# Attention: reciprocal sums applied to the exponents on GpSimd, value products with the latents stationary

## The reference

```python
def one_block(qi):
    s = jnp.einsum('bqhd,bkhd->bhqk', qi, k).astype(jnp.float32) * scale
    p = jax.nn.softmax(s, axis=-1).astype(v.dtype)
    return jnp.einsum('bhqk,bkhd->bqhd', p, v)
```

## Time and profile before

| What | Value |
|---|---|
| Median of 3 runs | 2599.09 us (2598.75 to 2599.27) |
| Profiled execution: its own time | 2597.56 us |
| Profiled execution: span | 2595.8 us |
| TensorE busy in the span | 93% |
| VectorE, ScalarE, GpSimd busy | 30%, 20%, 9% |
| Attention loop, layer 0 and layer 1 | about 303 us each (328 to 631, 1588 to 1891) |

### The profile page before, as it was taken

One profiled execution on the slowest core, in us unless ns is written; L12 is line 12 of the kernel. 1 busy time (PEld: TensorE's weight loads), 2 busy tenths in 40 slices (PEclk: granted clock), 3 DMA queues, 4 the chain that ended last, 5 costly groups with the idle time before them and its releaser, 6 DMA issues.

```text
span 2595.8 us, 33714 instructions
## 1 busy us (share of the span) xinstructions
PE 2427.0 (93%) x13939; PEld 1630.1 (63%) x13939; DVE 790.1 (30%) x1662; ACT 508.1 (20%) x1024; POOL 233.8 (9%) x371
## 2 busy tenths in 40 slices
PE   6999999999995899999979999999999949999994
PEld 4545566666443778888744455666654447887873
DVE  2401344454237211111142023454533451111112
ACT  2310121222233111101141002122213321111112
POOL 2000010100000121111200000000000002112121
PEclk8999999999997899999989999999999969999997
DMA  9100223311225588888840003330012258888887
GB/s 316 33 21 0 82 86 111 131 66 43 73 97 186 164 275 276 276 278 274 271 137 16 21 0 99 113 104 28 1 68 98 98 182 274 272 268 279 275 277 242
DMA packets 163074, 383.65 MB, mean 148 GB/s; under 512 B 12944, under 2 KB 23416, under 8 KB 162976
## 3 DMA queue, kind: packets, MB, share of 16 engines
q1 hardware_dynamic: 142944, 332.51, 37.4%
q0 software_dynamic: 20032, 49.77, 7.5%
HBM read 334.63 MB, written 47.61 MB: 147 GB/s over the span
## 4 chain that ended last, share of the span: by engine, by line
PE 91%; DVE 4%; DMA 2%; SPq 1%; ACT 1%; issue 1%; DVEq 0%; POOLq 0%; ACTq 0%
PE PS L1213 11%; PE PS L1220 11%; PE PS L1078 11%; PE PS L1240 9%; PE PS L815 8%; PE PS L975 7%; PE PS L908 6%; PE PS L769 5%; PE PS L758 5%; PE PS L957 4%; PE PS L920 4%; PE PS L1234 2%; PE PS L869 1%; PE PS L933 1%; PE PS L1198 1%; DVE top_i L1812 1%
## 5 line engine op out<-in xcount | busy, mean ns | idle before, releaser
L1213 PEld LDWEIGHTS PS<-r,ring 128*128 128x128 f32 x2048 | 285.8, 192 | 18.6 <-issue 18.6
L1213 PE MATMUL PS<-r,ring 128*128 128x160 f32 x2048 | 287.9, 302 | 3.5 <-ACT r L1457 3.5
L1078 PE MATMUL PS<-ring,mix 128*128 128x512 f32 x640 | 288.4, 598 | 1.2 <-DVE mix L1694 1.2
L1220 PE MATMUL PS<-r,ring 128*128 128x160 f32 x2048 | 283.4, 299 | 0.0
L1220 PEld LDWEIGHTS PS<-r,ring 128*128 128x128 f32 x2048 | 279.9, 190 | 0.0
L1240 PE MATMUL PS<-ring,r 128*128 128x512 f32 x512 | 228.3, 599 | 0.0
L908 PE MATMUL PS<-lat,r 128*128 128x512 f32 (+1 forms) x416 | 205.5, 579 | 5.4 <-ACT r L1342 2.7
L815 PE MATMUL PS<-r,ring 128*128 128x512 f32 (+1 forms) x576 | 208.4, 521 | 1.6 <-ACT r L1299 1.6
L975 PE MATMUL PS<-r 128*128 128x128 f32 x1536 | 202.2, 276 | 0.0
L975 PEld LDWEIGHTS PS<-r 128*128 128x128 f32 x1536 | 188.1, 192 | 18.9 <-issue 18.7
L1078 PEld LDWEIGHTS PS<-ring,mix 128*128 128x128 f32 x640 | 116.4, 190 | 129.7 <-issue 129.7
(11 more groups left out here) (259 smaller groups left out, 2171.8 us busy)
## 6 DMA issues: line engine op xcount, KB each, us to landing
ring<-in_w_gate_dram SPq DMA_DIRECT2D x32, 2048.0 KB, 9.9
ring<-in_w_up_dram SPq DMA_DIRECT2D x32, 2048.0 KB, 10.4
ring<-in_w_down_dram SPq DMA_DIRECT2D x32, 2048.0 KB, 9.6
ring<-in_w_ada_dram SPq DMA_DIRECT2D x21, 2048.0 KB, 20.9
x_dram<-r SPq DMA_DIRECT2D x20, 512.0 KB, 2.9
r<-x_dram SPq DMA_DIRECT2D x20, 512.0 KB, 4.1
r<-in_x_sample_dram SPq DMA_DIRECT2D x16, 512.0 KB, 4.1
ring<-in_w_in_dram SPq DMA_DIRECT2D x4, 2048.0 KB, 9.8
```

What stands on the lines that cost most here:

```text
L1078: ins = pe.matmul(psum(2 * (s % 2) + n, 512), mix[:, k, tile * P:(tile + 1) * P], W_OUT[n][:, k, :], start=(k == 0), stop=(k == KD - 1))
L1213: ins = pe.matmul(PS[:, b // 2, (b % 2) * 256:(b % 2) * 256 + SLOTS], W_G[:, k, b * P:(b + 1) * P], XST[par][:, k, :], start=(k == 0), sto ...
L1220: ins = pe.matmul(PS[:, 2 + b // 2, (b % 2) * 256:(b % 2) * 256 + SLOTS], W_U[:, k, b * P:(b + 1) * P], XST[par][:, k, :], start=(k == 0), ...
```

## The change

The reciprocals of the row sums are applied to the exponents, before they are turned, and no longer to the outputs. `invert_sum` only signals `inv_ready`; it stands after `row_max(n, 1)` for slot 0 and, for slot 1, after the first `copy_turned` of the next iteration. GpSimd multiplies `Pr[slot]` by `pinv` in place, 512 columns a round (two pieces of 256 for prompt tiles), and signals `p_scaled` for each round, on which `turn` waits. In `times_values` the operands are exchanged: `CKVT` is stationary, `PTr` moves, so that the result has the latent's numbers on partitions, as `mix` wants it. `scale_out`, `OS` and `turn_out` fall away, and `copy_out` copies each slot from bank 7. The stores of the gates move from GpSimd to SP, each behind the load of the piece of weights two later. The order of copies in the tail is adapted.

```diff
...
         SHUF = r2[:, 6144:7168]
-        OS = r2[:, 7168:7680].rearrange("p (s i c) -> p s i c", s=2, i=2)
         W_A = r2[:, 8192:9216].rearrange("p (h k c) -> p h k c", h=HEADS, k=2)
...
         o_summed = sem("o_summed")
-        o_scaled = sem("o_scaled")
-        o_turned = sem("o_turned")
+        inv_ready = sem("inv_ready")
+        p_scaled = sem("p_scaled")
         o_copied = sem("o_copied")
...
                 sp.wait_ge(ada_zeroed, l + 2)
+                def store_gate(i):
+                    la, n = ADA_ITEMS[l][i]
+                    if n in ADA_GATES:
+                        sp.wait_ge(ada_biased, 1 + ADA_AT[l] + i + 1)
+                        for g in range(2):
+                            for j in range(4):
+                                sp.dma_start(mod_dst[la, g, n, j:j + 1, :], ada_s[i % 2][32 * j + g:32 * j + g + 1, :])\
+                                    .then_inc(ada_stored[i % 2], 16)
                 for i, (la, n) in enumerate(ADA_ITEMS[l]):
...
                             .then_inc(ada_landed[i % 2], 16)
+                    if i >= 2:
+                        store_gate(i - 2)
+                for i in range(len(ADA_ITEMS[l]) - 2, len(ADA_ITEMS[l])):
+                    store_gate(i)
                 sp.wait_ge(ada_summed, 1 + ADA_AT[l + 1] - 1)
...
                 pool.memset(ada_b[1], 0.0).then_inc(ada_zeroed, 1)
-                for i, (la, n) in enumerate(ADA_ITEMS[l]):
-                    if n in ADA_GATES:
-                        pool.wait_ge(ada_biased, 1 + ADA_AT[l] + i + 1)
-                        for g in range(2):
-                            for j in range(4):
-                                pool.dma_start(mod_dst[la, g, n, j:j + 1, :], ada_s[i % 2][32 * j + g:32 * j + g + 1, :])\
-                                    .then_inc(ada_stored[i % 2], 16)
+                def scale_exponents(n, slot):
+                    pool.wait_ge(inv_ready, at(l, 2 * NI, 2 * n + slot + 1))
+                    for r in range(rounds_of(n)):
+                        if ITEMS[n][1] is PROMPT_TILES:
+                            for i in range(PT):
+                                e = Pr[slot][:, i * NP:(i + 1) * NP]
+                                ins = pool.tensor_scalar(e, e, pinv[:, 2 * slot + i:2 * slot + i + 1], None, ALU.mult)
+                        else:
+                            e = Pr[slot][:, 512 * r:512 * (r + 1)]
+                            ins = pool.tensor_scalar(e, e, pinv[:, 2 * slot:2 * slot + 1], None, ALU.mult)
+                        ins.then_inc(p_scaled, 1)
+                for n in range(NI):
+                    for slot in range(2):
+                        scale_exponents(n, slot)
                 for i in range(2):
...
                     k = turned(n, slot, r)
-                    pe.wait_ge(exp_done, at(l, 2 * NI, 2 * n + slot + 1))
+                    pe.wait_ge(p_scaled, at(l, ROUNDS, k))
                     if k > 1:
                         pe.wait_ge(pt_ready, at(l, ROUNDS, k - 1))
-                    if n and slot == 1 and r == 0:
-                        pe.wait_ge(o_copied, at(l, NI, n))
                     if slot == 0 and r == 0 and 0 < n <= len(ADA_ITEMS[l]):
...
                     if r == 0 and 2 * n + slot > 0:
-                        pe.wait_ge(o_scaled, at(l, 2 * NI, 2 * n + slot))
+                        pe.wait_ge(o_copied, at(l, 2 * NI, 2 * n + slot))
                     for j in range(4):
...
                             ins = pe.matmul(PS[:, 7, slot * 256 + (j // 2) * P:slot * 256 + (j // 2 + 1) * P],
-                                            PTr[slot][:, j, :], CKVT[:, j % 2, :], start=(j % 2 == 0), stop=(j % 2 == 1))
+                                            CKVT[:, j % 2, :], PTr[slot][:, j, :], start=(j % 2 == 0), stop=(j % 2 == 1))
                         else:
-                            ins = pe.matmul(PS[:, 7, slot * 256:slot * 256 + P], PTr[slot][:, k, :], CKVT[:, PT + k, :],
+                            ins = pe.matmul(PS[:, 7, slot * 256:slot * 256 + P], CKVT[:, PT + k, :], PTr[slot][:, k, :],
                                             start=(k == 0), stop=(k == 11))
...
                         ins.then_inc(o_summed, 1)
-
-                def turn_out(n):
-
-                    if n < 0:
-                        return
-                    tiles = PT if ITEMS[n][1] is PROMPT_TILES else 1
-                    pe.wait_ge(o_scaled, at(l, 2 * NI, 2 * n + 2))
-                    done = turned(n + 1, 1, 0) - 1 if n + 1 < NI else ROUNDS
-                    pe.wait_ge(pt_ready, at(l, ROUNDS, done))
-                    for slot in range(2):
-                        for i in range(tiles):
-                            c = (slot * tiles + i) * P
-                            ins = pe.transpose(PS[:, 6, c:c + P], OS[:, slot, i, :], ident[:, :])
-                    ins.then_inc(o_turned, 1)
...
                         rotary_scores(n, c)
-                    turn_out(n - 2)
                     times_values(n - 1, 0, 2)
...
                 n = NI - 1
-                pe.wait_ge(o_copied, at(l, NI, NI - 2))
+                pe.wait_ge(o_copied, at(l, 2 * NI, 2 * (NI - 2)))
                 pe.wait_ge(exp_done, at(l, 2 * NI, 2 * n + 1))
...
                 turn(n, 0, 2)
-                turn_out(n - 1)
                 times_values(n, 0, 1)
...
                 times_values(n, 1, 2)
-                pe.wait_ge(o_copied, at(l, NI, NI - 1))
+                pe.wait_ge(o_copied, at(l, 2 * NI, 2 * (NI - 1)))
                 value_heads(8)
                 value_heads(9)
-                turn_out(n)
-                pe.wait_ge(o_copied, at(l, NI, NI))
+                pe.wait_ge(o_copied, at(l, 2 * NI, 2 * NI))
                 value_heads(10)
...
                 pe.wait_ge(mod_ready, 2 * l + 2)
-                pe.wait_ge(o_scaled, at(l, 2 * NI, 2 * NI))
                 for s in range(NT):
...
-                def copy_out(n):
+                def copy_out(n, slot):
...
                     tiles, t0 = (PT, 0) if t is PROMPT_TILES else (1, t)
-                    act.wait_ge(o_turned, at(l, NI, n + 1))
-                    act.activation(mix[:, 2 * p:2 * p + 2, t0 * P:(t0 + tiles) * P],
-                                   psum(6, 2 * tiles * P).rearrange("p (h q) -> p h q", h=2), ACT.Copy)\
-                        .then_inc(o_copied, 1)
+                    act.wait_ge(o_summed, at(l, 2 * NI, 2 * n + slot + 1))
+                    act.activation(mix[:, 2 * p + slot, t0 * P:(t0 + tiles) * P], PS[:, 7, slot * 256:slot * 256 + tiles * P],
+                                   ACT.Copy).then_inc(o_copied, 1)
...
                 for n in range(NI):
-                    copy_out(n - 2)
+                    copy_out(n - 1, 0)
                     exponents(n, 0)
+                    copy_out(n - 1, 1)
                     exponents(n, 1)
                 copy_value_heads(0)
-                copy_out(NI - 2)
-                for m in (2, 4, 6, 8):
-                    copy_value_heads(m)
-                copy_out(NI - 1)
+                copy_value_heads(2)
+                copy_out(NI - 1, 0)
+                copy_value_heads(4)
+                copy_value_heads(6)
+                copy_out(NI - 1, 1)
+                copy_value_heads(8)
                 copy_value_heads(10)
...
                     dve.wait_ge(exp_done, at(l, 2 * NI, 2 * n + slot + 1))
-                    step(dve.reciprocal(pinv[:, c:c + m], psum_row[:, c:c + m]))
-
-                def scale_out(n, slot):
-
-                    if n < 0:
-                        return
-                    tiles = PT if ITEMS[n][1] is PROMPT_TILES else 1
-                    c = 2 * slot
-                    dve.wait_ge(o_summed, at(l, 2 * NI, 2 * n + slot + 1))
                     if n:
-                        dve.wait_ge(o_turned, at(l, NI, n))
-                    for i in range(tiles):
-                        ins = dve.tensor_scalar(OS[:, slot, i, :], PS[:, 7, slot * 256 + i * P:slot * 256 + (i + 1) * P],
-                                                pinv[:, c + i:c + i + 1], None, ALU.mult)
-                    ins.then_inc(o_scaled, 1)
+                        dve.wait_ge(p_scaled, at(l, ROUNDS, turned(n - 1, slot, rounds_of(n - 1) - 1)))
+                    dve.reciprocal(pinv[:, c:c + m], psum_row[:, c:c + m]).then_inc(inv_ready, 1)
...
                 for n in range(NI):
-                    for r in range(3):
-                        copy_turned(n - 1, 0, r)
-                    invert_sum(n - 1, 0)
-                    scale_out(n - 1, 0)
+                    copy_turned(n - 1, 0, 0)
+                    invert_sum(n - 1, 1)
+                    copy_turned(n - 1, 0, 1)
+                    copy_turned(n - 1, 0, 2)
                     copy_turned(n - 1, 1, 0)
...
                     copy_turned(n - 1, 1, 2)
-                    invert_sum(n - 1, 1)
                     row_max(n, 1)
+                    invert_sum(n, 0)
```

(6 more changed lines are left out.)

## The result

The changed kernel takes 2612.22 us (median of 6 runs, 2610.54 to 2613.7) against 2598.92 (6 runs) before: ratio 1.0052, 95% interval 1.0039 to 1.0065. That is 13.3 us or 0.52% slower: beyond the range, and on the side of rival 1. The profiled execution took 2610.54, its span 2608.5, which is 12.7 more than before's 2595.8; traces are compared by span.

What follows compares the result with a forecast made beforehand. TensorE, busy 98% of layer 0's attention window, was taken as the bound. Layer 0's -3.55 and layer 1's -0.95 made -4.5 us, 2597.56 to 2593.1; the median, 1.5 higher, was forecast at 2594.6, range 2590 to 2605.

Steps and rivals of the forecast that it cites:

- rival 1: GpSimd is slow: sixteen hand-overs carry the multiply, each 0.1 us costs 1.6; at 1.3 us, 2605; chance 0.2 for over 0.2% slower.
- the price of the multiply: GpSimd's `scale_exponents`, 128x512 elements a round: 0.65 us, bounds 0.5 and 1.3, from rows of a copy and selects.
- `turn_out`, 0.2 an item: TensorE's two transpositions between rotary scores and slot 0's last value products fall away: 0.2 us gained per item.
- Iteration 10, 1.0 each layer: `turn_out` just before `turn(9, 1, 0)`, which waited for the copy out of bank 6, falls away: 1.0 us gained.
- The hand-overs of 0.15 each: Semaphore hand-overs around GpSimd's multiply, 0.15 us in and 0.15 out, making 0.95 us from reciprocal to `turn`.
- The ordinary item's stall: Items without modulation product: first turn 6.71 us after `turn(.., 1, 1)`, not 6.16; stall 0.55, less 0.2 gain, +0.35 an item.
- Modulated items hidden until the multiply passes 2 us: Items with a modulation product: a cover of 1.4 us hides the multiply until it passes 2 us; they gain 0.2.
- First item +0.3: First, prompt item of each layer: reciprocal 0.2, hand-overs 0.3, two 256-column multiplies of 0.4 delay its turn: +0.3 us.
- Layer 1, iterations 9 and 10, +0.4: No modulation there: `turn(10, 0, 0)` at about 1777.7 against 1777.31, +0.4 us for both iterations, gain included.
- Bias add, 0.1 in iteration 2: The bias add follows one more reciprocal, at the first item and in iteration 10 of layer 0: +0.1 us each.
- The tail, -2.4 a layer: End of each layer: `turn_out` and two scalings fall away, 1.2 + 0.85 + 0.35 = 2.4 us gained, bounds 1.9 and 2.7.
- rival 3: Tail gives only two visible idle times (0.88, 0.47) because VectorE's copies bound it: 2596.7; with the forecast, chance 0.5 for no change.

Runs made afterwards that it cites:

- experiment 2: Changed kernel without GpSimd's multiplies and VectorE's wait for them; the turn waits for the exponents, reciprocals left out of the result: 2584.49 us, ratio 0.9949.
- experiment 3: Changed kernel with VectorE multiplying slot 0's first round right after its reciprocal, GpSimd all other rounds: 2590.0 us, ratio 0.9969.
- experiment 10: Changed kernel with scores (n, 0, 1) ahead of the first turn and VectorE multiplying slot 0's first round: 2591.94 us, ratio 0.9974.
- experiment 7: As experiment 3, but GpSimd's rounds of slot 0 wait for VectorE's multiply: 2591.46 us, ratio 0.9971.
- experiment 11: Changed kernel with GpSimd multiplying by the constant 1.0 instead of the column of reciprocals: 2607.58 us (one run).

## Why the prediction was wrong

**The step that failed** is the price of the multiply, "I take 0.65 us; the upper bound is twice that, 1.3". Its two anchors were a copy and a select, whose rows both ran near 0.85 ns an element; neither is arithmetic in f32. The multiply takes 1.566, above even the upper bound, which had no row behind it but a factor of two. That is over the 1 us that the prediction named as a sign of being wrong. The two sides of the sum show where the error sits: its gains add up to 13.6 us (the items, iteration 10 of each layer, the tails) and experiment 2 measured 13.5 in the attentions, while the waits and other costs were put at 9.1 and took 13.5 + 12.65 = 26.1. The Trainium skill (GPSIMD Engine Reference, sections 3.1 and 4.1) was right in direction, but its factor of two against VectorE is 3.2 in these runs, and its roughly line rate for one input holds for the copy, not for this multiply.

**The step that carries it** held. Rival 1 said that sixteen hand-overs carry the multiply. Ordered by the time from GpSimd's start to the first round's end, the spans are

| first round on GpSimd | us | span | two attentions, against before |
|---|---|---|---|
| none | 0 | 2581.5 | -13.5 |
| copy | 0.61 | 2590.3 | -7.0 |
| multiply by a constant (one run) | 1.49 | 2605.5 | +8.7 |
| multiply, as changed | 1.57 | 2608.5 | +12.65 |
| in two halves | 1.84 | 2612.5 | +17.9 |

From copy to multiply it is 18.2/0.96 = 19 us of span for a microsecond, against 16 forecast; the gain is gone at 0.61 + 5.5/19 = 0.90, where the rival said 0.93. By the attentions alone it is 20, and 0.95. Its formula at the true length gives -4.5 + 16 x 0.92 = +10.2; measured +12.7, of which 1.4 is the clock. The 4.0 us from the constant to the column are more than 0.07 us a hand-over can carry: 1.5 lie around iteration 11 of layer 1, where the clock fell in the latter alone, and an ordinary item grows by 0.13, 0.08 in its wait (1.07 to 1.15) and 0.05 from the turn to the next rotary scores (5.17 to 5.22).

**Point by point.**
- `turn_out`, 0.2 an item: 0.17 to 0.18. Right.
- Iteration 10, 1.0 each layer: there without GpSimd's step (15.59 against 16.57 in layer 0, 13.82 against 15.04 in layer 1), half of it kept by the changed kernel in layer 0 and none in layer 1. Right in what is removed, wrong in what is kept: the wait for the multiply comes in the same place.
- The reciprocal 5.76 after the turn: exact. The hand-overs of 0.15 each: 0.10 and 0.05, so 0.15 too dear together. The ordinary item's stall is therefore 0.55 + 0.92 - 0.15 = 1.32, by the timeline 7.47 - 6.16 = 1.31. Less 0.17 of gain, and 0.1 behind the restart (the next turn starts 1.55 after, 584.20, where it is 1.47 in experiment 2): +1.24 against +0.35.
- Modulated items hidden until the multiply passes 2 us: right as far as tried, 18.71 with every length up to 1.84.
- First item +0.3: +1.24, for it has two multiplies of 0.92 where 0.4 each was taken.
- Layer 1, iterations 9 and 10, +0.4: +3.4 (0.9 and 2.5). The 0.9 is the wait of 0.84 for the two multiplies of the prompt item 9, a hand-over that the prediction counted for the first item alone. The 2.5 is about the wait of 2.02 and the 1.4 of the clock, which no step of the prediction spoke of, less the 1.0 won.
- Bias add, 0.1 in iteration 2: +0.5, as the changed kernel keeps TensorE waiting 0.28 there for GpSimd; without GpSimd's step it is nothing (15.53 against 15.55).
- The tail, -2.4 a layer: -2.2 beside its own stall of 1.24. Right; rival 3 (1.35 a layer) is refuted.
- Operand exchange, stores by SP: zero, both measured by themselves.

**Where the 12.7 went**, by the differences of the starts: nine ordinary items in the loops +11.4 (1.24 each, and 0.3 more in one where VectorE started late); the same hand-over at the head of the two tails +2.5; first items +2.5; iteration 2 of both layers +1.0; iterations 10 to 12 of layer 1 +4.3, of layer 0 -1.1; the other items, modulated or with a prompt `turn_out`, -3.5; the tails' own gain -4.4. That sums to 12.7.

## What to carry to other kernels

The price of an operation on GpSimd is not to be taken from a copy or a select there: look for a row of arithmetic with the same type, or bound it by the same operation on VectorE times three or more. When scaling moves ahead of a consumer, only the first piece that the consumer waits for is on the path; give that one to the fast engine and the rest can stay slow (here 2590.0 against 2612.2). And an order that gives TensorE cover in front of one wait takes it from another: count the gap behind each of the moved groups.

## What the runs showed of the hardware

- GpSimd, f32 from SBUF to SBUF: copy 606 ns for 128x512 and 395 for 128x256 (0.82 ns an element), multiply by a column 1566 and 924, by a constant 1491 and 852 (both 2.5 ns an element). VectorE: the multiply 482.
- A semaphore from VectorE started GpSimd 0.10 us after the reciprocal's end, and one from GpSimd started TensorE's turn 0.05 after the multiply's.
- Of VectorE's and GpSimd's multiplies that overlap, the one that starts later is stretched. In experiment 3 VectorE's took 0.83 instead of 0.49 when it began 0.13 behind GpSimd's. So it did once in experiment 10 (0.83, 0.13 behind). Where VectorE's began first by 0.06, five of GpSimd's took 8.02 instead of the 7.73 of experiment 7, and one multiply took up to 1857 ns:

```profile
L631 POOL TENSOR_SCALAR r<-r,pinv x160: 1556/1562/1857, 346.5 to 1895.9; 128x512 f32<-128x512 f32 x160
```

The Trainium skill (SBUF — State Buffer, section "Who interferes with whom") says that GpSimd and VectorE share a pair of ports, which a VectorE `tensor_scalar` can take in its two-port modes, and that whichever starts second then blocks until the first has finished. The trace agrees that they disturb one another, but not with the size: GpSimd's multiply, begun at 578.72, would have ended at about 580.3, and VectorE's had already ended at 579.68.
- TensorE's granted clock fell to its lower level after a wait of 2.02 us that followed one of 0.64, and was 1.00 again from 1789.40. Waits of 0.64 and 1.94 (experiment 11) left it at 1.00, as did single waits of 1.0 to 1.2 us in every ordinary item.
